# Two transformer blocks, one core: where the norm's operand lies in on-chip memory

## What is computed

```
for i in range(2):                                   # first block
    h = mixer_block(h, norm_mix[i], w_in[i], ...)    # u = rmsnorm(h); proj = u @ w_in  (1024 x 9280)
    u = rmsnorm(h, norm_ffn[i])
    h = h + (swiglu(u, gate, up, down) if i == 0     # 1024 x 2816, twice, and back
             else moe(u, router, 8 experts, top 2))
    h = h + sigmoid(rmsnorm(h) @ w_ple_gate[i]) * (p[i] @ w_ple[i])
for l in range(2):                                   # second block
    u = rmsnorm_2(x, norm1_g[l]) @ w_in_2[l]         # 1024 x 3648
    x = x + mix(u) @ w_out_2[l]
    x = x + square(relu(rmsnorm_2(x, norm2_g[l]) @ w_up[l])) @ w_down[l]   # 1024 x 4096 and back
```

## Time and profile before

| | |
|---|---|
| median of three runs | 2141.46 us (2141.18 to 2144.6) |
| the profiled execution, first to last instruction | 2140.0 us; no other time of this execution is given |
| PE (TensorE) busy | 2083.7 us, 97% |
| VectorE, ScalarE, GpSimd busy | 72%, 64%, 3% |
| matmuls | 15388, of them 6720 with the norm's tile moving |
| bytes from memory | 186 GB/s over the span |

### The profile page before, as it was taken

How to read it: one execution, slowest core, us unless ns; L and a number is a source line. 1 busy time by engine, 2 the same in 40 slices (tenths; PEclk the granted TensorE clock), 3 DMA queues, 4 the chain that set the end, 5 groups by cost and what they waited for, 6 DMA issues and landing times.

```text
span 2140.0 us, 37171 instructions
## 1 busy us (share of the span) xinstructions
PE 2083.7 (97%) x15388; PEld 1944.3 (91%) x15388; DVE 1531.2 (72%) x2200; ACT 1361.4 (64%) x1879; POOL 65.4 (3%) x102
## 2 busy tenths in 40 slices
PE   8999999999999989999999999999999999999999
PEld 7988999999989889998888888888889999979999
DVE  6777556766577675566999899977868665876664
ACT  5765575554567755657777777776766545776553
POOL 0013000000000130000000000000000000000000
PEclk9999999999999999999999999999999999999999
DMA  7424345565554343455999999954415565524554
GB/s 272 149 95 139 99 155 175 180 193 188 169 172 153 96 142 98 150 183 189 337 331 334 334 333 333 349 192 151 131 60 179 189 194 163 158 70 138 190 191 133
DMA packets 126448, 400.59 MB, mean 187 GB/s; under 512 B 26048, under 2 KB 26432, under 8 KB 126272
## 3 DMA queue, kind: packets, MB, share of 16 engines
q1 hardware_dynamic: 126272, 398.14, 56.0%
HBM read 395.72 MB, written 2.36 MB: 186 GB/s over the span
## 4 chain that ended last, share of the span: by engine, by line
PE 81%; ACT 8%; DVE 7%; issue 2%; POOL 2%; DMA 1%; SPq 0%; ACTq 0%; DVEq 0%; POOLq 0%
PE ps L493 80%; DVE wlo L2186 2%; ACT whi L1409 2%; ACT arena L1419 2%; ACT scr L1419 2%; DVE arena L2194 1%; ACT L1419 1%; DVE arena L2186 1%; POOL arena L3166 1%; ACT L1413 1%; DVE scr L2186 1%; POOL arena L3169 1%; DVE h L2186 1%; ACT rst L1419 1%; PE ps L1086 0%
## 5 line engine op out<-in xcount | busy, mean ns | idle before, releaser
L2186 DVE TENSOR_TENSOR wlo<-raw,whi 128x1024 fp32r<-128x1024 f32 (+2 forms) x622 | 745.5, 1212 | 283.7 <-ACT whi L1409 278.5
L1409 ACT ACTIVATE whi<-raw 128x1024 fp32r<-128x1024 f32 (+2 forms) x622 | 643.1, 1042 | 321.9 <-PE ps L493 315.2
L493 PE MATMUL ps<-uh,whi 128*128 128x256 f32 x2240 | 644.2, 288 | 10.9 <-DVE arena L2194 4.2
L493 PE MATMUL ps<-uh,wlo 128*128 128x256 f32 x2240 | 632.2, 282 | 0.0
L493 PE MATMUL ps<-ul,whi 128*128 128x256 f32 x2240 | 625.8, 279 | 0.0
L493 PE MATMUL ps<-arena_r,whi 128*128 128x256 f32 x2720 | 473.4, 279 | 2.9 <-DVE arena_r L2186 2.0
L493 PEld LDWEIGHTS ps<-uh,whi 128*128 128x128 f32 x2240 | 420.2, 188 | 23.9 <-issue 14.6
L493 PEld LDWEIGHTS ps<-ul,whi 128*128 128x128 f32 x2240 | 421.8, 188 | 4.2 <-issue 3.8
L493 PEld LDWEIGHTS ps<-uh,wlo 128*128 128x128 f32 x2240 | 419.4, 187 | 0.0
L493 PEld LDWEIGHTS ps<-arena_r,whi 128*128 128x128 f32 x2720 | 411.6, 188 | 5.8 <-DVE arena_r L2186 3.4
L493 PE MATMUL ps<-arena_r,wlo 128*128 128x256 f32 x1360 | 376.7, 277 | 0.0
(11 more groups left out here) (186 smaller groups left out, 2186.8 us busy)
## 6 DMA issues: line engine op xcount, KB each, us to landing
raw<-stream SPq DMA_DIRECT2D x586, 512.0 KB, 4.2
arena<-stream SPq DMA_DIRECT2D x64, 512.0 KB, 5.6
CO<-stream SPq DMA_DIRECT2D x44, 512.0 KB, 5.4
raw<-stream SPq DMA_DIRECT2D x32, 384.0 KB, 4.4
arena<-stream SPq DMA_DIRECT2D x20, 384.0 KB, 4.3
CO<-stream SPq DMA_DIRECT2D x12, 384.0 KB, 4.6
CO<-const SPq DMA_DIRECT2D x3, 683.0 KB, 6.9
h<-xT SPq DMA_DIRECT2D x4, 256.0 KB, 6.4
```

The lines of the kernel that those rows point to most:

```text
L493: return self.e.matmul(o, l, r, start=start, stop=stop, skip_group_check=True)
L1409: self.e.activation(M.whi[:, b:b + n], M.raw[a][:, 0:n], ACT.Copy).then_inc(K.sem("weight_hi"), 1)
L2186: return self.e.tensor_tensor(o, a, b, op)
```

## The change

The two buffers `uh` and `ul` become one, `u`, of 4672 elements. `Tiles` now takes the shift of tile 7 as an argument: the high part begins at element 80 with a shift of 200, the low part at 2384 with a shift of 232. The built program puts `u` at 84256, and so tiles 0 to 6 of both parts begin at 608 modulo 1024, tile 7 at 384 in the high and at 512 in the low part, as before. For two tiles at once the view is now taken from the end, since the shift of tile 7 is larger. The experts' second pair of gathered operands keeps its former places in the buffer (352 and 480 modulo 1024). The scratch for descriptors of software DMAs, which this program does not use, shrinks from 16384 to 1024 bytes to make room. That moves every other buffer: `whi`, `wlo`, `raw` and `h` by -15360 bytes, `arena_r` by -13312, all of them multiples of 1024. `M.mixp`, the operand of the second block's output projection, has its high part at 96 and its low part at 608. The instructions of every engine, their order and what they wait for are the same.

```diff
@@
+PARTS = ((80, 200), (2384, 232))
+NORMED = 4672
@@ class Tiles
-    def __init__(self, ap, c0=0, c1=T):
-        self.ap, self.c0, self.c1 = ap, c0, c1
+    def __init__(self, ap, step=STEP, c0=0, c1=T):
+        self.ap, self.step, self.c0, self.c1 = ap, step, c0, c1
@@
-            n = T + (STEP if k.stop == 8 else 0)
-            return v3(self.ap[p, k.start * T:k.start * T + 2 * n], n)[:, :, c0:c1]
-        at = k * T + (STEP if k == 7 else 0)
+            n = T + (self.step if k.stop == 8 else 0)
+            return v3(self.ap[p, (k.start + 2) * T + n - T - 2 * n:(k.start + 2) * T + n - T], n)[:, :, n - T + c0:n - T + c1]
+        at = k * T + (self.step if k == 7 else 0)
@@ class Memory
-        self.h, uh, ul = sb("h", 2048), sb("uh", 2048 + 2 * OFF, F32R), sb("ul", 2048 + 2 * OFF, F32R)
-        self.hT, self.U = v3(self.h), tuple(Tiles(x[:, OFF:2048 + 2 * OFF]) for x in (uh, ul))
+        self.h, u = sb("h", 2048), sb("u", NORMED, F32R)
+        self.hT, self.U = v3(self.h), tuple(Tiles(u[:, at:at + 2048 + n], n) for at, n in PARTS)
@@
-        self.UG = [[Tiles(ARr[...]) for i in range(2)], self.U]
+        self.UG = [[Tiles(ARr[...]) for i in range(2)],
+                   [Tiles(u[:, OFF + i * (2048 + 2 * OFF):(i + 1) * (2048 + 2 * OFF)]) for i in range(2)]]
@@ def kernel
-    nc = bacc.Bacc("TRN2", target_bir_lowering=False, num_devices=1)
+    nc = bacc.Bacc("TRN2", target_bir_lowering=False, num_devices=1,
+                   dynamic_dma_scratch_size=1024)
```

More of the change, by code:

```diff
@@ L192, in __getitem__ @@
             assert k.stop == k.start + 2 and k.start % 2 == 0
-            n = T + (STEP if k.stop == 8 else 0)
-            return v3(self.ap[p, k.start * T:k.start * T + 2 * n], n)[:, :, c0:c1]
-        at = k * T + (STEP if k == 7 else 0)
+            n = T + (self.step if k.stop == 8 else 0)
+            return v3(self.ap[p, (k.start + 2) * T + n - T - 2 * n:(k.start + 2) * T + n - T], n)[:, :, n - T + c0:n - T + c1]
+        at = k * T + (self.step if k == 7 else 0)
         return self.ap[p, at + c0:at + c1]
     def columns(self, c0, c1):
-        return Tiles(self.ap, c0, c1)
+        return Tiles(self.ap, self.step, c0, c1)
 class Steps:
@@ L347, in __init__ @@
         at = 4096 + OFF
-        self.UG = [[Tiles(ARr[:, at + i * (2048 + 2 * OFF):at + (i + 1) * (2048 + 2 * OFF)]) for i in range(2)], self.U]
+        self.UG = [[Tiles(ARr[:, at + i * (2048 + 2 * OFF):at + (i + 1) * (2048 + 2 * OFF)]) for i in range(2)],
+                   [Tiles(u[:, OFF + i * (2048 + 2 * OFF):(i + 1) * (2048 + 2 * OFF)]) for i in range(2)]]
         at += 2 * (2048 + 2 * OFF)
```

## The result

| | before | after |
|---|---|---|
| median (lowest to highest) | 2141.32 us (2140.09 to 2144.6), 4 runs | 2151.7 us (2149.46 to 2152.38), 4 runs |
| ratio of the times, 95% interval | | 1.0047 (1.0028 to 1.0065) |
| profiled execution, first to last instruction | 2140.0 us | 2147.7 us |
| its own time | not given | 2149.46 us |

The changed kernel is slower by 0.47%, about 10 us, and the interval lies clear of the 0.2% that can be told from no change. The forecast was 2127.1 us, with a range of 2117 to 2138: wrong in sign and outside its range. In the changed kernel the line of `mm` is 496, and both parts of the norm's operand are called `u`.

The account below looks back on a forecast made before the run. PE's matmul rate was taken to bound the kernel. Gains on the chain of 13.8 us (tiles 0 to 6 behind a tile 7) and 0.6 us (the others), all else 0, made 2141.5 - 14.4 = 2127.1 us, range 2117 to 2138.

Parts of the forecast that it names:

- What bounds the kernel: Whole kernel: PE busy 97% of the span and 81% of the chain, so the matmul rate sets the time.
- Two lasting rates at 608: Matmul streams with the moving operand at 608: 340 or 353 ns a triple, decided by how the stream was entered.
- Tiles 0 to 6 of a block that follows a tile 7 directly: Norm's matmuls: 3865 become 4.2 ns faster each, 16.2 us, of which 13.8 on the chain.
- Other buffers move by multiples of 1024, so I count nothing: Moved buffers such as `arena_r`: fast stretches stand at odd and even multiples of 1024 alike, so 0 us.
- far bound of +13 us: `arena_r`: the cost if moving the buffers lost its fast rate, some 2850 matmuls x 4.6 ns.
- Tile 7 at 359: Norm's tile 7, 280 triples: stays at 359 ns a triple, 0 us, with bounds of -5 to +5 us.
- One in seven of the others fast: Norm's 2015 matmuls behind pauses, float32 work or the values: one in seven fast, 1.2 us, 0.6 on the chain.
- What lies on the chain: Norm's matmuls during waits for other engines gain nothing, leaving 13.8 and 0.6 us; all of it would be 17.4.
- The residue is not the cause: Rival for the norm's tiles: only `arena_r` may have the fast rate, so no gain, 2141.5 us; chance 0.11.
- one-way kick: Rival: tile 7 makes slow streams fast but fast ones slow, so every second block is fast, 2134 us; chance 0.12.
- Tile 7's rate locks in: Rival: the norm's stream keeps tile 7's 359 ns for the block, 11.4 us lost, 2153 us; chance 0.07.
- More than the sum: Rival: norm's tiles are fast after pauses too and filler counts, 24.7 us gained, 2117 us; chance 0.08.

Follow-up runs that it names:

- e1: The kernel before, with only the descriptor scratch reduced so that every buffer moves by -15360 bytes; 2142.47 us, 0.9996.
- e4: The changed kernel with tile 6 put back at 352/480, tile 7 still at 384/512, tiles 0 to 5 at 608; 2131.53 us, 0.9938.
- f4: The changed kernel with tiles 5 and 6 at 352/480, tile 7 at 384/512, tiles 0 to 4 at 608; 2130.74 us, 0.9953.
- g1: The changed kernel with tile 0 at 352/480, tile 1 at 384/512, tiles 2 to 7 at 608, `arena_r` at 608; 2129.06 us, 0.9937.
- g2: The changed kernel with tiles 0 and 1 at 352/480, tile 2 at 384/512, tiles 3 to 7 at 608, `arena_r` at 608; 2129.02 us, 0.9944.
- e2: The kernel before without the shift of tile 7, so all eight tiles at 352/480; 2148.49 us, 1.0029.
- e3: The changed kernel with tile 7 at 608 as well, so all eight tiles of both parts there; 2144.98 us, 1.0009.
- g3: The kernel before with the shared buffer alone moved by 96 bytes, `arena_r` from 608 to 704; 2155.42 us, 1.0071.
- f1: The changed kernel with tile 0 at 352/480, tile 1 at 384/512, tiles 2 to 7 at 608, `arena_r` unintentionally at 704; 2139.33 us, 0.9993.
- f3: The changed kernel with tiles 0 to 2 at 352/480, tile 3 at 384/512, the rest at 608, `arena_r` unintentionally at 704; 2141.02 us, 0.9998.

## Why the prediction was wrong, point by point

- **What bounds the kernel: right.** The rate at which matmuls follow each other decides, and nothing else moved: same chain, same work of the other engines.
- **Two lasting rates at 608, decided by how a stretch is entered: right**, and it is what the whole loss hangs on.
- **The step that failed** is "Tiles 0 to 6 of a block that follows a tile 7 directly", 3865 x 4.2 = 16.2 us, of which 13.8 on the chain. It took from 11 entries of 11 that tile 7 makes a stream at 608 fast, and from there went to "tile 7 seems to forget what was before it". All 11 had tiles at 352/480 ahead of tile 7. In the changed kernel no block of `proj_T` has, and through tile 7 0 of 171 slow blocks became fast. The norm's term came out at 6500 x 0.20 = 1.3 us gained. The argument offered for forgetting was that a stream at 352/480 reaches its own rate from any history; but that place has only one rate, so it could not show anything about history.
- **"Other buffers move by multiples of 1024, so I count nothing"**: right about the addresses (e1), wrong as a whole, since the same setter served `arena_r`. Losing it cost 4027 x 2.37 = 9.5 us. The far bound of +13 us was the right size under the wrong heading, and should have been tied to tile 7: if it does not set the rate in the norm's blocks, it does not set it in `arena_r` either. The prediction put the failure of the step at 0 gained when it was a loss.
- **Tile 7 at 359: wrong**, 354. With slow tiles at 608 ahead of it the intervals of 121.5 ns disappear from it together with the setting, and the slow triple is the next tile 0 at 360. The first interval of 117 ns that the prediction gave a block behind a tile 7 is seen only where the pair set the rate (117.5 in e4). Whether the slower tile 7 is part of the setting is not shown.
- **One in seven of the others fast: right in size.** In the changed kernel 14 of 82 entries of the norm's behind a pause or float32 matmuls are fast (entries with at least nine matmuls before the next pause or tile 7).
- **What lies on the chain: not contradicted.** It was put at 14.4 of 17.4 us, 83%. In the four kernels that gained (e4, f4, g1, g2) 79 to 87% of the rate term arrived in the time, but with intervals of 3 to 5 us these shares would also allow all of it, and in those that lost they run from 67% (e2) to 122% (the changed kernel).
- **The residue: half right.** 608 does allow the fast rate for the norm's operand, outside `arena_r` too. "The residue is not the cause" falls with e3, e4 and g1. But the argument against it that "an operand with its high part at 96 runs at 353" was one rate read as the only one: that operand runs at 340 for 52 triples in a row in the changed kernel, twice, and once each in e1, e2, e4 and g1. It makes the same mistake as the failed step, a reading from one history.
- **The rivals.** The one-way kick had its second half right: a fast stream at 608 is thrown out by tile 7, 6 of 6. It had the first half wrong. "Tile 7's rate locks in", at 2153 us, ended next to the measured 2151.7, but by another way: no stream ran at 359, they ran at 353, and the time was lost in `arena_r`. Its price held none of that, though its chance was given together with "a lost `arena_r` rate"; that the numbers meet is luck. (Its break-even is also off: 89 ns won against 41 lost balance at about seven blocks in ten, not six.) Slower had a chance of 0.07; it was too little, since every gain and the present good state hung on one unseen transition.
- **What the idea is worth** once the setting pair is kept: 2129 us in g1 and g2, near the forecast of 2127.1, with blocks of the norm's at 2.75 to 2.77 us, near the 2.74 that was forecast. "More than the sum", 2117, was reached by no kernel.

What stays open: by what means the chip comes to two rates, why in e4 the first pair behind a pause often fails, and all places but those named. The places seen fast (608, and 96 with 608) both lie 96 bytes past a multiple of 512, and those never seen fast do not; that 512 is the period is a guess, which no run was made to test. Whether more pairs, or a pair at entries into `arena_r` behind pauses, would gain more was not tried.

## What to carry to other kernels

When a stretch is fast, find out what made it so before moving anything near it: the detail to be improved here (the norm's tiles at a "slow" place) was part of what made the next product fast. An effect seen 11 times of 11 has been seen for one history only if all 11 share it; the transition that the change creates has to be in the trace, or the forecast needs a case that loses what is there now. And a change in a buffer's size moves what lies behind it: 96 bytes cost the kernel before about 15 us (g3, 1.0071).

## What the runs showed of the hardware

- Matmuls with 256 moving float32r columns, alternating with weight loads, follow each other at 113.3 or 117.7 ns (340 or 353 a triple) at the same granted clock of 1.00, PE busy throughout, and a stream keeps its rate over hundreds of matmuls. The place of the moving operand modulo 1024 bytes decides whether the fast rate can occur (608, and 96 for the high with 608 for the low part: yes; 352/480 and 704: never seen), the matmuls before decide whether it does.
- At 704 the same down projection ran at 117.3 ns an interval in f1 to f3 and at 118.7 in g3: more than one lasting rate there too, none of them 113.3.
- The fast rate was set dependably by going from 352/480 to 384/512 to 608 in consecutive triples (11 of 11 entries in before, e1, e4, f4, g2; 9 of 11 in g1), never directly from 352/480 (e2, 0 of 11) and never from slow 608 over 384/512 (0 of 171). Behind pauses it comes now and then, about one time in six (14 of 82 in the changed kernel), and no run shows what decides.
- The Trainium skill (TensorE: Matmul & The Clock Gate, "Back-to-back issue gap") gives one warm gap for an isolated matmul of a number of columns, for 256 an estimate of 109 ns by its formula, and for a stream with weight loads one spacing each for 128 and for 512 columns; neither depends on a place or on what ran before. These traces do not agree: they show 113.3 and 117.7 ns for 256 columns and, at 704, 117.3 to 120.0, over all of `arena_r` in g3 118.5. Between 113.3 and 118.5 lie, as an estimate, 5.2 ns x 4027 = 21 us for `arena_r` alone.
